# Branch A of a fused encoder block: 64 row products against two groups of seven block products, merged by accumulating DMA

## The chip, the core and the metric

One NeuronCore of a Trainium2 chip runs the whole layer in one launch. The metric is the time of one execution in microseconds (us) on the device. The engines are TensorE (PE, matmul; PEld is its weight load), VectorE (DVE), ScalarE (ACT), GpSimd (POOL) and SyncE (SP), which only issues DMAs. Each engine works through its own list of instructions in order; they meet at semaphores only.

## What is computed

One encoder layer, 512 tokens of width 1024, float32. One projection of the normalised input feeds three token mixers: A (sliding-window attention, 16 heads), X (cross-attention into 256 memory tokens) and P (pooling). Then

```
ya = oa @ w_branch_a          # (512 x 1024) @ (1024 x 1024)
yx = ox @ w_branch_x          # (512 x 512) @ (512 x 1024)
yp = op @ w_branch_p          # (512 x 512) @ (512 x 1024)
merged = gate_a * ya + gate_x * yx + gate_p * yp
x = x + rms_norm(merged @ w_out, norm_mix_post)
h = rms_norm(x, norm_ffn_pre)
x = x + rms_norm((silu(h @ w_gate) * (h @ w_up)) @ w_down, norm_ffn_post)
```

The gates are sigmoids of 3 x 1024 further columns of the input projection. The change concerns `ya` and the merging.

## The kernel before

**Precision.** Every float32 operand is kept as two float32r parts: `hi` is a rounded copy (ScalarE, `Copy`), `lo` is the rest (VectorE, subtract). A product is three matmuls, hi*hi, hi*lo and lo*hi (`three`, L1944). So each weight tile passes SP (load), ScalarE (`split_hi`, L469), VectorE (`split_lo`, L482) and TensorE.

**The stream.** `plan` (L92) lists `steps`: memory rows, k, v, q, qx, pin, 12 gate tiles, P tiles 0 to 3, X tiles 0 to 7, then A tiles 0 to 3, P tiles 4 to 7, A tiles 4 to 7. A step of A is one tile of 128 output channels by 512 tokens, 8 slices of 128 inputs, so 24 matmuls of 512 columns. A step of P or X is two tiles of 4 slices each. `stream` is the order of weight loads: two entries are one 1 MB chunk, in one of two `raw` buffers (`load_chunk`, L623); the chunks of the output projection (`out`) are mixed in between. Splits run up to two steps ahead (`stream_upto`, L495); `wait_split_free` (L413) says when a destination is free.

**Units.** Twelve attention units (8 of A, 4 of X) are laid over steps 15 to 38, two steps each: scores, maxima, exponentials, `normalise` (L1413), transposes (L2075) and output (L2085).

**Late groups.** Twelve of the gate tiles (A 0 to 7 and P 4 to 7) are computed in three late groups ahead of step A0 (44, `LATE`, L66) by a seven-product scheme: a 2 x 2 block product with 7 block products instead of 8 (`products`, L80; `late_product`, L2105). Its operands are blocks of the weights (A11 to A22) and sums of them (S1 to S4, VectorE, `late_weight_sum` L1469), blocks of the tokens (B11 to B22) and sums of these (T1 to T4). The T sums are made by POOL (L845 to L862) from `hT_hi` and `hT_lo`; POOL starts on them when the last A unit and the last `map` tile are done. ScalarE splits them in `token_hi` (L967) at steps A0-4 and A0-3. The intermediate results U1, U2 and U3 are copied from PSUM by ScalarE (`late_keep`), and VectorE adds them to the block results (`late_block_out`). One block product is 2 x 4 x 3 = 24 matmuls of 256 columns. The feed-forward uses the same scheme.

**Merging.** For each tile VectorE multiplies the PSUM tile by its gate (`merge`, L1437, into `part`) and adds it to the running sum in `gates` (L1451). For an A tile this is the last addition: ScalarE then makes `mrg_hi` (L951) and VectorE `mrg_lo` (L1460), two steps later in their lists.

**Output projection.** L2187: token rows t = 0 to 3; in row t = 0 each slice k waits for its weights `wo_hi[k]`, `wo_lo[k]` and for `mrg_split`; 6 matmuls of 512 columns per k and t. SP reloads x into `x1` when all tiles are done (L712), then the two gains and the first feed-forward chunks.

**POOL.** Besides the T sums: the pooling mixer (L834 to L840, four groups), the row norms (`inverse_rms`), and a few sums later. It issues no DMA in this kernel.

The lines that matter for memory: `op_hi` lies at 176 KB and `op_lo` at 184 KB of each partition (read by the P tiles), `late_sum` at 192, `part` and `late_U2` at 200, `late_U1` at 204, `gates` at 72 to 96, `hT_hi` and `hT_lo` at 40 to 72.

Of the kernel before, what the change touches and what calls it, by code (L numbers as in the profile page):

```python
# [65 lines left out]
LATE = (("a", 0), ("a", 4), ("p", 4))  # L66
# [25 lines left out]
def plan():  # L92
# [17 lines left out]
    steps += [[("a", j)] for j in range(4)] + halves("p", 4) + [[("a", j)] for j in range(4, KT)]  # L110
# [15 lines left out]
def encoder_block(nc, x, x_t, mem_t, g_mix_pre, g_mix_post, g_mem, w_in, rel_bias, sinks, w_mem_kv, w_pool_map,  # L126
# [9 lines left out]
    A0 = steps.index([("a", 0)])  # L136
# [67 lines left out]
    out_at = [40, 48, 56, 64, 72, 80, 88, 196]  # L204
    wo_hi = [sb(f"wo_hi{k}", a, [P, D], F32R) for k, a in enumerate(out_at)]
    wo_lo = [sb(f"wo_lo{k}", a + 4, [P, D], F32R) for k, a in enumerate(out_at)]
# [64 lines left out]
    rel_dram = nc.dram_tensor("rel_scratch", [A_HEADS, 192], F32, kind="Internal").ap()  # L271

# [6 lines left out]
    with ExitStack() as ctx:  # L279
# [14 lines left out]
        for n, t in enumerate(tiles):  # L294
# [7 lines left out]
            if A0 <= step < A0 + 4:  # L302
                b = (step - A0 + 2) % 4
# [18 lines left out]
        x_again = [sem(f"x_again{i}") for i in range(TT)]  # L322
# [18 lines left out]
        sigmoid_ready, mixed_ready, mrg_hi_done, mrg_split = (sem(n) for n in ("sigmoid_ready", "mixed_ready", "mrg_hi_done", "mrg_split"))  # L341
# [10 lines left out]
        late_sigmoid = sem("late_sigmoid")  # L352
        ops_hi, ops_split, product_done = sem("ops_hi"), sem("ops_split"), sem("product_done")
# [13 lines left out]
        def chunk_halves(first):  # L367
# [7 lines left out]
            else:  # L375
# [6 lines left out]
                if t == "a":  # L382
                    v, col = wa_v, P * i
                elif t == "gate":
# [28 lines left out]
        def wait_split_free(eng, s):  # L413
# [6 lines left out]
            elif kind == "out" and n < 4:  # L420
                eng.wait_ge(late_done, OPS * len(LATE))
            elif kind == "out":
                eng.wait_ge(tile_full, len(tiles))
                eng.wait_ge(mrg_split, KT)
            elif kind == "ffn" and n < 3:
                eng.wait_ge(tile_full, len(tiles))
# [169 lines left out]

        def both(name):

            return pair["CDAB".index(name)][:, :, 0:2 * P]
# [12 lines left out]
        def _(sp):  # L612
# [97 lines left out]
            for c in range(late_chunk + 1, last_out + 1):  # L710
                load_chunk(c)
            sp.wait_ge(tile_full, len(tiles))  # L712
            for t in range(TT):
                sp.dma_start(x1[:, t, :], x[P * t:P * t + P, :]).then_inc(x_again[t], 16)
# [61 lines left out]
        def _(pool):  # L776
# [46 lines left out]
            pool.wait_ge(pads_ready, 6)  # L823
            for g, w in enumerate(POOL_WINDOWS):
# [17 lines left out]
            pool.wait_ge(o_full, A_UNITS)  # L842
            pool.wait_ge(tile_full, tile_no[("map", 3)] + 1)
# [6 lines left out]
            def token_diff(dst, a, b):  # L850
# [11 lines left out]
                .then_inc(late_t_made, 1)  # L862

# [23 lines left out]
        def _(act):  # L887
# [61 lines left out]
            def merged_hi(j):  # L949
                act.wait_ge(mixed_ready, j + 1)  # L950
                act.activation(mrg_hi[:, j, :], mix_slot(j), ACT.Copy).then_inc(mrg_hi_done, 1)  # L951
# [91 lines left out]
            for s in range(NS):  # L1043
# [6 lines left out]
                if s >= 2 and steps[s - 2][0][0] == "a":  # L1050
                    merged_hi(steps[s - 2][0][1])
# [45 lines left out]
            for j in (KT - 2, KT - 1):  # L1097
                merged_hi(j)
# [212 lines left out]
        def _(dve):  # L1311
# [125 lines left out]
            def merge(t):  # L1437
# [4 lines left out]
                if kind == "a" or (kind == "p" and j >= 4):  # L1442
                    dve.wait_ge(late_sigmoid, 2 * [k for k, at in LATE].index(kind) + (2 * (j // 4) + 2 if kind == "a" else 2))
                else:
                    dve.wait_ge(sigmoid_ready, (j if kind == "p" else 4 + j) // 2 + 1)
                onto = kind == "a" or (kind == "p") == (j >= 4)
                dst = part[:, :] if onto else gate_slot(kind, j)
                dve.tensor_tensor(dst, bk(bank_of[n]), gate_slot(kind, j), ALU.mult).then_inc(tile_merged, 1)
                if onto:
                    dve.wait_ge(tile_merged, merged_no[t])  # L1450
                    ins = dve.tensor_tensor(mix_slot(j), mix_slot(j), part[:, :], ALU.add)  # L1451
                    if kind == "a":
                        ins.then_inc(mixed_ready, 1)
                        dve.wait_ge(mixed_ready, j + 1)
                    else:
                        link(ins)

            def merged_lo(j):
                dve.wait_ge(mrg_hi_done, j + 1)
                dve.tensor_tensor(mrg_lo[:, j, :], mix_slot(j), mrg_hi[:, j, :].bitcast(F32), ALU.subtract)\  # L1460
                   .then_inc(mrg_split, 1)

# [130 lines left out]
            for s in range(NS):  # L1593
# [9 lines left out]
                if s >= 2 and steps[s - 2][0][0] == "a":  # L1603
                    merged_lo(steps[s - 2][0][1])
# [29 lines left out]
                if s >= 1 and not A0 - 6 < s <= A0:  # L1634
                    for t in steps[s - 1]:
# [4 lines left out]
                        elif t[0] in "axp":  # L1640
# [13 lines left out]
                if s == MEM_TURNS + 1:  # L1654
                    for e in range(E_X, E_V):
# [6 lines left out]
                        ins.then_inc(turned_split, 1)  # L1662
            for t in steps[NS - 1]:
                merge(t)
            for j in (KT - 2, KT - 1):
                merged_lo(j)
# [24 lines left out]
            for t in range(TT):  # L1691
                if t >= 1:
                    h2_lo(t - 1)
                dve.wait_ge(x_again[t], 16)
# [248 lines left out]
        def _(pe):  # L1943
# [16 lines left out]
            def tile(t, s, midway=None):  # L1960
# [13 lines left out]
                if A0 <= s < A0 + 4:  # L1974
# [13 lines left out]
                if kind in ("a", "p", "x"):  # L1988
                    xhi, xlo = {"a": (oa_hi, oa_lo), "p": (op_hi, op_lo), "x": (ox_hi, ox_lo)}[kind]
                else:  # L1990
                    xhi, xlo = hT_hi, hT_lo
                if kind == "a":
                    pe.wait_ge(o_split, A_UNITS)
# [139 lines left out]

# [253 lines left out]
```

## Time and profile before

| | us |
|---|---|
| runs of the kernel | 778.16, 779.55, 780.31 (median 779.55) |
| the profiled execution | 778.36 |
| its span in the profile | 776.6 |
| TensorE busy | 767.9 (99%) |
| VectorE, ScalarE, POOL busy | 575.4, 377.5, 90.7 |
| DMA | 85.76 MB, mean 110 GB/s |

The span is 1.8 us shorter than the execution's own time; start and end lie around it. In a record of a matmul the duration includes the pipeline's length, so the pace is read from the distance of two starts, not from the duration.

### The profile page before, as it was taken

The page shows a single profiled execution, that of the slowest core. Times are in us where ns is not written, and L with a number is a line of the kernel's source. Part 1 is how long each engine was busy: PE and PEld are TensorE (multiplying, and loading weights), DVE is VectorE, ACT ScalarE, POOL GpSimd, SP SyncE. Part 2 cuts the span into 40 slices and gives each one's busy share as a digit, 9 for nine tenths or more (in the row PEclk, how much of TensorE's full clock was granted, in tenths as well). Part 3 has the DMA queues.
Part 4 walks back from the last instruction along what each step waited for, and adds up shares of the span by engine and source line. Part 5 has one row for each costly group of instructions (what it writes and reads, how often), then busy time and mean ns, then how long its engine had stood idle before and what let it go on. Part 6 is the DMA issues. An engine that isn't in the chain of part 4 may idle for free.

```text
span 776.6 us, 11895 instructions
## 1 busy us (share of the span) xinstructions
PE 767.9 (99%) x4670; PEld 677.6 (87%) x4670; DVE 575.4 (74%) x643; ACT 377.5 (49%) x598; POOL 90.7 (12%) x139
## 2 busy tenths in 40 slices
PE   8999999999999999999999999999999999999997
PEld 7888778777877899988888999999999999888885
DVE  6666566676745788867655598888888888999897
ACT  7733445444337445553243565544445445675462
POOL 5120001334910000000001110000011110000002
PEclk9999999999999999999999999999999999999999
DMA  8862213213211333244371013333333346214102
GB/s 298 304 199 73 90 56 100 63 55 98 66 54 59 105 109 107 84 136 151 120 270 55 5 52 110 109 108 108 108 108 108 108 135 216 108 57 166 50 1 108
DMA packets 68070, 85.76 MB, mean 110 GB/s; under 512 B 3504, under 2 KB 57536, under 8 KB 68032
## 3 DMA queue, kind: packets, MB, share of 16 engines
q1 hardware_dynamic: 67568, 84.71, 33.3%
q8 instruction: 26, 0.43, 0.2%
q10 hardware_dynamic: 464, 0.53, 0.2%
q14 instruction: 12, 0.10, 0.0%
HBM read 83.12 MB, written 2.11 MB: 110 GB/s over the span
## 4 chain that ended last, share of the span: by engine, by line
PE 98%; DMA 1%; ACT 0%; DVE 0%; DVEq 0%; issue 0%; POOLq 0%; SPq 0%; POOL 0%; ACTq 0%
PE pair L1950 91%; PE pair L2082 1%; PE pair L2064 1%; PE pair L2096 1%; PE pair L2071 1%; PE pair L2101 1%; DMA memT_in<-in_mem 1%; PE pair L1957 0%; PE pair L1978 0%; PE pair L2032 0%; PE pair L2160 0%; PE pair L2171 0%; PE pair L2177 0%; DVE x L1677 0%; ACT square L901 0%; DVEq L279 0%
## 5 line engine op out<-in xcount | busy, mean ns | idle before, releaser
L1950 PE MATMUL pair<-hT_hi,w_hi 128*128 128x512 f32 x240 | 98.1, 409 | 0.0
L493 DVE TENSOR_TENSOR w_lo<-raw,w_hi 128x1024 fp32r<-128x1024 f32 x52 | 70.5, 1356 | 35.6 <-ACT w_hi L480 35.5
L1950 PE MATMUL pair<-hT_hi,w_lo 128*128 128x512 f32 x240 | 93.8, 391 | 0.0
L1950 PE MATMUL pair<-hT_lo,w_hi 128*128 128x512 f32 x240 | 93.6, 390 | 0.0
L1950 PE MATMUL pair<-T_hi,op_lo 128*128 128x256 f32 x320 | 90.6, 283 | 0.0
L1950 PE MATMUL pair<-T_hi,op_hi 128*128 128x256 f32 x320 | 90.6, 283 | 0.0
L1950 PE MATMUL pair<-T_lo,op_hi 128*128 128x256 f32 x320 | 90.6, 283 | 0.0
L480 ACT ACTIVATE w_hi<-raw 128x1024 fp32r<-128x1024 f32 x52 | 54.8, 1056 | 49.9 <-PE pair L1950 30.8
L1950 PE MATMUL pair<-B_hi,op_lo 128*128 128x256 f32 x240 | 67.9, 283 | 0.0
L1950 PE MATMUL pair<-B_hi,op_hi 128*128 128x256 f32 x240 | 67.9, 283 | 0.0
L1950 PE MATMUL pair<-B_lo,op_hi 128*128 128x256 f32 x240 | 67.9, 283 | 0.0
L1950 PEld LDWEIGHTS pair<-T_hi,op_hi 128*128 128x128 f32 x320 | 61.4, 192 | 0.0
L1950 PEld LDWEIGHTS pair<-T_hi,op_lo 128*128 128x128 f32 x320 | 61.4, 192 | 0.0
L1950 PEld LDWEIGHTS pair<-T_lo,op_hi 128*128 128x128 f32 x320 | 61.4, 192 | 0.0
L1950 PEld LDWEIGHTS pair<-hT_hi,w_hi 128*128 128x128 f32 x240 | 45.1, 188 | 10.4 <-issue 1.0
L1950 PEld LDWEIGHTS pair<-hT_hi,w_lo 128*128 128x128 f32 x240 | 45.0, 188 | 9.8
L1950 PEld LDWEIGHTS pair<-hT_lo,w_hi 128*128 128x128 f32 x240 | 45.1, 188 | 9.7 <-issue 1.0
L800 POOL TENSOR_SCALAR meansq<-part_meansq 128x1 f32<-128x1 f32 x16 | 5.7, 356 | 358.1 <-ACT square L901 357.8
L1950 PEld LDWEIGHTS pair<-B_hi,op_hi 128*128 128x128 f32 x240 | 46.1, 192 | 0.0
L1950 PEld LDWEIGHTS pair<-B_hi,op_lo 128*128 128x128 f32 x240 | 46.1, 192 | 0.0
L1950 PEld LDWEIGHTS pair<-B_lo,op_hi 128*128 128x128 f32 x240 | 46.1, 192 | 0.0
L1147 ACT ACTIVATE U<-pair 128x512 f32<-128x512 f32 x30 | 17.9, 598 | 57.6 <-PE pair L1950 57.6
(273 smaller groups left out, 2051.1 us busy)
## 6 DMA issues: line engine op xcount, KB each, us to landing
raw<-in_w_in SPq DMA_DIRECT2D x42, 512.0 KB, 4.8
raw<-in_w_ffn_up SPq DMA_DIRECT2D x22, 512.0 KB, 4.8
raw<-in_w_ffn_gate SPq DMA_DIRECT2D x22, 512.0 KB, 4.2
W<-in_w_ffn_down SPq DMA_DIRECT2D x8, 1024.0 KB, 5.0
raw<-in_w_branch_a SPq DMA_DIRECT2D x8, 512.0 KB, 4.0
raw<-in_w_out SPq DMA_DIRECT2D x8, 512.0 KB, 3.7
raw<-in_w_ffn_down SPq DMA_DIRECT2D x6, 512.0 KB, 4.2
raw<-in_w_mem_kv SPq DMA_DIRECT2D x4, 512.0 KB, 6.9
```

The lines of the kernel that those rows point to most:

```text
L480: eng.activation(hi, src, ACT.Copy).then_inc(weights_hi, 1)
L493: eng.tensor_tensor(lo, raw_view(s), hi.bitcast(F32), ALU.subtract).then_inc(weights_split, 1)
L800: link(pool.tensor_scalar(meansq[:, n:n + 1], part_meansq[:, c:c + 1], 1.0, EPS, ALU.mult, ALU.add))
L1147: act.activation(kept[u][:, :, :], both("A"), ACT.Copy).then_inc(kept_ready, 1)
L1950: ins = pe.matmul(dst, a, b, start=first and n == 0, stop=last and n == 2, skip_group_check=onto)
L2064: ins = pe.matmul(scores[:, pr // 2, at:at + KEYS], q[lo:lo + 64, 2 * a + pr % 2, ch, :, :].rearrange("p j t -> p (j t)"), k_dup[lo:lo + 6 ...
L2071: ins = pe.matmul(scores[:, i // 2, at:at + N_MEM], qx[:, a, P * i:P * i + P], mk[:, a, :], start=True, stop=True)
L2082: ins = pe.transpose(turned[:, at // 4, P * (at % 4):P * (at % 4) + P], probs[:, i, :], ident[:, :])
L2096: ins = pe.matmul(bk(O_BANK)[64 * half:64 * half + 64, 2 * P * c:2 * P * c + 2 * P], v_c[:, 2 * b + c, 64 * a:64 * a + 64], probs[:, i:i + ...
L2101: ins = pe.matmul(bk(O_BANK), mv[:, m, a, :], probs[:, 4 * m:4 * m + 4, :], start=(m == 0), stop=(m == MT - 1))
```

## The change

Branch A leaves the list of steps. P tiles 4 to 7 become the last steps, and `ya` is computed behind them in two groups (`BRANCH`, output channels 0 to 511 and 512 to 1023) of seven block products.

- The weights' sums S1 to S4 are made once, in DRAM, by POOL's DMAs: four copies, then four accumulating DMAs, two of them behind the pooling mixer. Signs are arranged so that only additions are needed.
- The tokens' sums T1 to T4 of `oa` are made by VectorE in `late_t` (steps 31 to 34), stored to DRAM by POOL, and loaded again by SP during the last late group. POOL's own T sums for the late groups come behind the stores.
- The operands are loaded block by block into four buffers `br_raw` (512 KB each), split by ScalarE and VectorE, in an order that is written out by hand along with everything else of this stretch.
- Each of the eight results (C11, C22, C21, C12 of a group) is formed by VectorE, multiplied by its gate, and added into `gates` by an accumulating DMA from SBUF to SBUF that POOL issues, each after the one before has landed. `merged_hi` and `merged_lo` then work on these blocks.
- The splits of the output projection's weights move: k=0 behind P tiles, k=1 to 5 into the second group, k=6 behind the last accumulation, k=7 behind the last `merged_lo`.

The diff, cut to its core:

```diff
-LATE = (("a", 0), ("a", 4), ("p", 4))
+LATE = (("p", 4), ("a", 0), ("a", 4))
+BRANCH = (0, 4)
+BLOCK_ORDER = ("C11", "C22", "C21", "C12")
-    steps += [[("a", j)] for j in range(4)] + halves("p", 4) + [[("a", j)] for j in range(4, KT)]
+    steps += halves("p", 4)
-    for c, at in ((1, n - 2), (0, n - 6)):
-        stream[at:at] = [("out", 2 * c), ("out", 2 * c + 1)]
-    stream += [("out", k) for k in range(4, KT)]
+    stream += [("out", k) for k in range(KT)]
+    br_raw = [sb(f"br_raw{i}", a, [P, 4, 2 * P]) for i, a in enumerate((192, 196, 184, 188))]
+    br_kept = {"U1": sb("br_U1", 204, [P, 2, 2 * P]), "U2": sb("br_U2", 202, [P, 2, 2 * P])}
+    br_kept["U3"] = br_kept["U1"]
+    br_out = {"C11": br_kept["U1"], "C22": sb("br_C22", 200, [P, 2, 2 * P]), "C21": br_kept["U3"], "C12": br_kept["U2"]}
+    out_at = [(80, 84), (72, 76), (40, 48), (44, 52), (56, 64), (60, 68), (196, 200), (88, 92)]
...
+            elif kind == "out" and n == 6:
+                eng.wait_ge(br_mixed, 16 * 8)
+                eng.wait_ge(br_split, 2 * OPS)
             elif kind == "out":
-                eng.wait_ge(tile_full, len(tiles))
-                eng.wait_ge(mrg_split, KT)
+                eng.wait_ge(mrg_split, 8)
...
+            def load_branch(n):
+                g, m = divmod(n, OPS)
+                name = products()[m][1]
+                if n < 2:
+                    sp.wait_ge(late_split, OPS * len(LATE))
+                elif n < 4:
+                    sp.wait_ge(tile_full, len(tiles))
+                else:
+                    sp.wait_ge(br_split, n - 3)
...
+                sp.dma_start(br_raw[n % 4][:, :, :], src).then_inc(block_ins[n % 4], 16)
+            sp.wait_ge(tok_stored, 64)
+            sp.wait_ge(late_done, OPS * len(LATE) - 3)
+            for b in TOKEN_SPLITS:
+                sp.dma_start(br_t[b][0][:, :, :], br_tok[b].rearrange("p (k n) -> p k n", k=4)).then_inc(tok_in, 16)
+            load_branch(0)
+            load_branch(1)
+            load_chunk(late_chunk + 2)
+            for n in range(2, 2 * OPS):
+                load_branch(n)
...
+            for name, a in (("S1", "A21"), ("S3", "A11"), ("S2", "A11"), ("S4", "A12")):
+                pool.dma_start(br_summed(name), br_block(a)).then_inc(br_copied, 16)
+            pool.wait_ge(br_copied, 64)
+            for name, b in (("S1", "A22"), ("S3", "A21")):
+                pool.dma_start(br_summed(name), br_block(b), accum_op=ALU.add, max_dma_last_dim=4096).then_inc(br_added, 16)
...
+            for b in range(4 * len(BRANCH)):
+                pool.wait_ge(br_gated, b + 1)
+                if b:
+                    pool.wait_ge(br_mixed, 16 * b)
+                pool.dma_start(br_part(gates, b), br_out[BLOCK_ORDER[b % 4]][:, :, :], accum_op=ALU.add).then_inc(br_mixed, 16)
...
+            def br_keep(g, u):
+                act.wait_ge(br_done, OPS * g + {"U1": 1, "U2": 3, "U3": 5}[u])
+                if u == "U3" or g:
+                    act.wait_ge(br_mixed, 16 * (4 * g + {"U1": -1, "U2": 0, "U3": 1}[u]))
...
+                act.activation(br_kept[u][:, :, :], both("A"), ACT.Copy).then_inc(br_kept_ready, 1)
+            def merged_hi(b):
+                act.wait_ge(br_mixed, 16 * b + 16)
+                act.activation(br_part(mrg_hi, b), br_part(gates, b), ACT.Copy).then_inc(mrg_hi_done, 1)
```

The order of ScalarE's list (VectorE's follows the same pattern, with the block results between):

```diff
+            br_operand_hi(0) ; br_token_hi("T2") ; br_token_hi("T1") ; br_operand_hi(1) ; br_operand_hi(2)
+            br_operand_hi(3) ; br_token_hi("T3") ; out_hi(0) ; br_keep(0, "U1") ; br_operand_hi(4) ; br_token_hi("T4")
+            br_operand_hi(5) ; br_keep(0, "U2") ; br_operand_hi(6) ; merged_hi(0) ; br_operand_hi(7) ; br_keep(0, "U3")
+            br_operand_hi(8) ; br_operand_hi(9) ; merged_hi(1) ; br_operand_hi(10) ; merged_hi(2) ; br_keep(1, "U1")
+            br_operand_hi(11) ; merged_hi(3) ; br_operand_hi(12) ; out_hi(1) ; br_keep(1, "U2") ; br_operand_hi(13)
+            merged_hi(4) ; out_hi(2) ; out_hi(3) ; br_keep(1, "U3") ; out_hi(4) ; out_hi(5) ; merged_hi(5)
+            merged_hi(6) ; out_hi(6) ; merged_hi(7) ; out_hi(7)
```

TensorE runs `branch_product` 14 times ahead of the output projection, in the order P1, P2, P6, P5, P7, P4, P3. P6 and P7 add onto the PSUM bank of P1 and wait for U1 and U2 to be kept; P3 adds onto that of P5 and waits for C22. In the output projection, row t = 0 waits for `mrg_split` 1, 3, 5 and 7 at k = 0, 2, 4 and 6, row t = 2 for 8.

## Rows read from the trace of the kernel before

**Rows 1.** The page: busy time, share of the span, instructions of each engine; chain by engine.
```profile
PE 767.9 (99%) x4670; PEld 677.6 (87%) x4670; DVE 575.4 (74%) x643; ACT 377.5 (49%) x598; POOL 90.7 (12%) x139
...
PE 98%; DMA 1%; ACT 0%; DVE 0%; DVEq 0%; issue 0%; POOLq 0%; SPq 0%; POOL 0%; ACTq 0%
```

**Rows 2.** The chain that ended last, in order of time: start us, us, what.
```profile
212.63 0.87 PE pair L2082 x8
...
247.83 162.81 PE pair L1950 x954
```

**Rows 3.** Busy time by stretch; then clock, DMA share, GB/s.
```profile
275.00:335.30 60.30, 60.30 (x505) 60.30 (x504) 51.03 (x51) 29.35 (x33) 0.00 (x0) 1.00 0.33 106
335.30:389.80 54.50, 54.50 (x243) 45.14 (x243) 36.04 (x43) 18.73 (x21) 0.00 (x0) 1.00 0.40 135
389.70:400.70 11.00, 11.00 (x49) 8.79 (x48) 7.37 (x8) 4.53 (x5) 0.00 (x0) 1.00 0.87 297
```

**Rows 4.** Timeline of TensorE: start us, us, instruction.
```profile
274.89 0.28 PE L1950 MATMUL pair<-hT_hi,late_op_hi 128*128 128x256 f32 x1
...
335.36 0.40 PE L1950 MATMUL pair<-oa_hi,w_hi 128*128 128x512 f32 x1
...
389.79 0.39 PE L1950 MATMUL pair<-wo_hi,mrg_hi 128*128 128x512 f32 x1
```

**Rows 5.** Busy time by stretch, columns as in rows 3: during the units.
```profile
72.00:98.00 26.00, 26.00 (x141) 20.53 (x139) 15.37 (x26) 12.08 (x40) 0.00 (x0) 1.00 0.26 81
```

**Rows 6.** Timeline of POOL from 140 us on.
```profile
148.29 3.02 POOL L834 TENSOR_TENSOR pooled<-pooled 128x512 f32<-128x512 f32 x2 [11.33 <-PE pair L1978]
...
194.05 5.74 POOL L847 TENSOR_TENSOR late_T<-hT_hi,hT_lo 128x1024 f32<-128x1024 f32 x2 [6.95 <-PE pair L1978]
...
213.98 3.23 POOL L861 TENSOR_TENSOR late_T<-late_T,late_T 128x1024 f32<-128x1024 f32 x1
401.93 0.19 POOL L800 TENSOR_SCALAR meansq<-part_meansq 128x1 f32<-128x1 f32 x1 [184.72 <-ACT square L901]
```

**Rows 7.** The page: DMA issues, KB each, us to landing.
```profile
raw<-in_w_in SPq DMA_DIRECT2D x42, 512.0 KB, 4.8
```

**Rows 8.** Timeline of VectorE, units 9 and 10.
```profile
205.04 2.15 DVE L1410 TENSOR_SCALAR neg_max<-row_max 128x4 f32<-128x4 f32 x1
...
209.40 2.26 DVE L1423 TENSOR_TENSOR probs<-probs,inv_denom 128x1024 f32<-128x1024 f32 x1
...
220.30 0.17 DVE L1410 TENSOR_SCALAR neg_max<-row_max 128x4 f32<-128x4 f32 x1
...
222.68 1.22 DVE L1423 TENSOR_TENSOR probs<-probs,inv_denom 128x1024 f32<-128x1024 f32 x1
```

**Rows 9.** Landing of L621 (320 to 390 us), L771 (result), L714 (x); one issue.
```profile
DMA to landing us min/median/max: 3.2/3.8/4.6
...
DMA to landing us min/median/max: 2.1/2.1/2.1
...
DMA to landing us min/median/max: 3.3/5.4/7.2
...
343.37 0.93 SPq L621 DMA_DIRECT2D raw<-in_w_branch_p  x2
```

**Rows 10.** Timelines of ScalarE, then VectorE; in brackets the idle time before and its end.
```profile
254.35 1.99 ACT L973 ACTIVATE late_T_hi<-late_T 128x1024 fp32r<-128x1024 f32 x2
...
329.80 0.60 ACT L977 ACTIVATE late_U<-pair 128x512 f32<-128x512 f32 x1 [2.32 <-PE pair L1950]
...
348.32 1.06 ACT L480 ACTIVATE w_hi<-raw 128x1024 fp32r<-128x1024 f32 x1 [1.09 <-DMA raw<-in_w_branch_p]
...
392.97 3.90 ACT L480 ACTIVATE wo_hi<-raw 128x1024 fp32r<-128x1024 f32 x4 [0.84 <-DVE mrg_lo L1460]
...
390.77 0.69 DVE L1451 TENSOR_TENSOR gates<-gates,part 128x512 f32<-128x512 f32 x1
...
394.06 4.63 DVE L493 TENSOR_TENSOR wo_lo<-raw,wo_hi 128x1024 fp32r<-128x1024 f32 x4 [1.21 <-ACT wo_hi L480]
```

More of the change, by code:

```diff
@@ L1441, in merge @@
                 dve.wait_ge(tile_full, n + 1)
[L1442 to L1443 removed]
+                if kind == "p" and j >= 4:
+                    dve.wait_ge(late_sigmoid, 2)
                 else:
                     dve.wait_ge(sigmoid_ready, (j if kind == "p" else 4 + j) // 2 + 1)
[L1446 removed]
+                onto = (kind == "p") == (j >= 4)
                 dst = part[:, :] if onto else gate_slot(kind, j)
@@ L1450, in merge @@
                     dve.wait_ge(tile_merged, merged_no[t])
[L1451 to L1460, printed above, removed]
-                   .then_inc(mrg_split, 1)
+                    link(dve.tensor_tensor(mix_slot(j), mix_slot(j), part[:, :], ALU.add))
@@ L1662, in _ @@
                         ins.then_inc(turned_split, 1)
+                if TOKENS_AT <= s < TOKENS_AT + 4:
+                    token_sums(s - TOKENS_AT)
+                if s == A0:
+                    br_operand_lo(0)
+                    br_token_lo("T2")
+            br_token_lo("T1")
+            br_operand_lo(1)
             for t in steps[NS - 1]:
                 merge(t)
-            for j in (KT - 2, KT - 1):
-                merged_lo(j)
+            br_operand_lo(2)
+            br_operand_lo(3)
+            br_token_lo("T3")
+            out_lo(0)
+            br_operand_lo(4)
+            br_token_lo("T4")
+            br_block_out(0, "C11")
+            br_operand_lo(5)
+            br_operand_lo(6)
+            merged_lo(0)
+            br_operand_lo(7)
+            br_block_out(0, "C22")
+            br_operand_lo(8)
+            br_block_out(0, "C21")
+            br_operand_lo(9)
+            merged_lo(1)
+            br_block_out(0, "C12")
+            br_operand_lo(10)
+            merged_lo(2)
+            br_operand_lo(11)
+            merged_lo(3)
+            br_block_out(1, "C11")
+            br_operand_lo(12)
+            out_lo(1)
+            br_operand_lo(13)
+            merged_lo(4)
+            out_lo(2)
+            out_lo(3)
+            br_block_out(1, "C22")
+            out_lo(4)
+            br_block_out(1, "C21")
+            out_lo(5)
+            merged_lo(5)
+            br_block_out(1, "C12")
+            merged_lo(6)
+            out_lo(6)
+            merged_lo(7)
+            out_lo(7)
+            done += KT
             def gained(t, h, n, number, y=y):
@@ L2132, in late_product, with branch_product @@
                 ins.then_inc(late_done, 1)
+            def branch_product(n):
+                g, m = divmod(n, OPS)
+                name, a, b, bank = products()[m]
+                pe.wait_ge(br_split, n + 1)
+                if name == "P1":
+                    if g:
+                        pe.wait_ge(br_kept_ready, 3 * g)
+                    else:
+                        pe.wait_ge(late_kept_ready, 3 * len(LATE))
+                        pe.wait_ge(o_split, A_UNITS)
+                if name == "P2" and g:
+                    pe.wait_ge(br_blocks, 4 * g - 3)
+                if name == "P5":
+                    if g:
+                        pe.wait_ge(br_blocks, 4 * g)
+                    else:
+                        pe.wait_ge(tile_merged, merged_no[tiles[-1]])
+                if name == "P6":
+                    pe.wait_ge(br_kept_ready, 3 * g + 1)
+                if name == "P7":
+                    pe.wait_ge(br_kept_ready, 3 * g + 2)
+                if name == "P3":
+                    pe.wait_ge(br_blocks, 4 * g + 2)
+                if g == 0 and b[0] == "T":
+                    pe.wait_ge(late_t_split, TOKEN_SPLITS.index(b) + 5)
+                (whi, wlo), xhi, xlo = br_op[n % 4], br_token(b, True), br_token(b, False)
+                fresh = name not in ("P6", "P7", "P3")
+                for i in range(2):
+                    for k in range(4):
+                        ins = three(both(bank)[:, i, :], whi[:, k, P * i:P * i + P], wlo[:, k, P * i:P * i + P],
+                                    xhi[:, k, :], xlo[:, k, :], fresh and k == 0, k == 3, onto=not fresh)
+                ins.then_inc(br_done, 1)
             def warm_up(n, bank):
```

227 lines of the change are left out of this document (189 added, 38 removed).

## The prediction

> **What bounds the kernel now.** I read the page first: TensorE is busy for 767.9 of 776.6 us and 98% of the chain that ended last is its own work [rows 1]. So only two things move the time: the matmul time in the stretch that is changed, and new idle time in front of a matmul. The chain in order of time shows 954 matmuls without a gap from 247.83 to 410.64 [rows 2]. This stretch holds the late gate groups, branch A, the last P tiles and the first row of the output projection. The granted clock there is 1.00 [rows 3]. VectorE is busy for 36.0 of 54.5 us and ScalarE for 18.7 [rows 3]: there is room, but both work through a fixed order, so the order decides.
>
> **What the change can gain.** The late groups run from 274.89 to 335.36: 60.47 us for 3 x 7 x 24 = 504 matmuls of 256 columns, 0.120 us each, so a block product takes 2.88 us. From 335.36 to 389.79 there are 240 matmuls of 512 columns, 0.2268 us each [rows 4]. Branch A is 8 x 8 x 3 = 192 of these: 43.5 us. Afterwards it is 2 x 7 x 24 = 336 of the short ones: 40.3 us. The gain is **3.2 us**, 0.41% of the time, and any wait of TensorE is taken from that. Counting 0.3% (2.3 us) as what a measurement can tell from no change, "faster" needs waits of less than 0.9 us in total.
>
> **What is moved ahead of 335 us, each at nothing, with its cover.**
> Weight sums: about 59 us POOL issues four 1 MB copies inside DRAM and waits for them, then two adds. Copies read and write 8 MB. Weight loads use 0.26 of the DMA engines at that time [rows 5]. At 100 GB/s the copies would last 80 us, to 139; POOL's next work starts at 148.29 [rows 6]. A weight load of 512 KB lands in 4.8 us [rows 7] and is issued two steps or more (14 us) before its split, so even a doubled landing is hidden. Without that cover each late chunk would cost TensorE its lateness.
> Token sums: eight VectorE operations of 1.2 us at steps 31 to 34 (185 to 217 us), in front of `normalise`. Before, unit 9's `normalise` ended at 211.66 and its transposes began at 212.63 [rows 2, 8]: only 1.0 us. But there VectorE was slowed by POOL's adds: the 2.26 us `normalise` takes 1.22 in unit 10, the 2.15 us `neg_max` 0.17 [rows 8]. POOL's adds now move behind the stores, so 3.0 us come back against 2.4 us of token work per step. Cost nothing.
> POOL's own chain for the late groups ran 194.05 to 217.21, 23.2 us [rows 6]. It now waits for the fourth sum (about 217) and the stores (5 us), so it runs from 222 to 246; ScalarE first wants its result at 254.35 [rows 10]. 8 us of slack; if it were gone, ScalarE's weight splits behind that wait would be late next. LATE's new order swaps equal groups. The `x_again` rename costs nothing. SP loads four token sums (2 MB) and operands 0 and 1 from about 328; P1 needs them only at 346.2 and P6 at 352.
>
> **The stretch from 335 us on.** P tiles 4 to 7 now come first: 48 x 0.2268 = 10.9 us, to 346.24. P1 and P2 follow to 352.0. Then:
>
> First wait, **P6**. Operands 2 and 3 go to `br_raw` at 184 to 192, where `op_lo` lies, so SP waits for the last P tile (its record ends 0.16 after its slot, 346.4). Loads there land 3.2 to 4.6 us after issue, median 3.8 [rows 9]; a pair issued at 343.37 let ScalarE start at 348.32, 4.95 later [rows 9, 10]. So operand 3 lands at about 351.4. ScalarE then does, in this order, operand 3, T3, output row 0 and only then keeps U1: 1.0 us each for the first three and 0.6 for U1 [rows 10]. U1 is there at 355.0; P6 adds onto the same PSUM bank and waits for it: **3.0 us**. With the fastest landing (3.2) still 1.5 to 2.3. Everything queued behind on ScalarE (operands 4, 5) keeps its lead.
>
> **The merging.** The last additions (0.69 us on VectorE [rows 10]) become eight accumulating transfers of 256 KB from SBUF to SBUF, issued by POOL one after the other, each after the previous landed. ScalarE waits for them in `merged_hi`, and its buffers U1, U2 and U3 wait as well. No row shows such a transfer. Nearest rows: a 256 KB store alone lands in 2.1 us; 512 KB loads in this stretch in 3.2 at least; the same under a burst in 5.4, up to 7.2 [rows 9]. The accumulation reads both operands, so its traffic is that of 512 KB; I take **3.2 us**, keep 2.1 and 5.4 as ends.
> The Trainium skill (DMA: Bandwidth & Descriptors, section Anatomy of one DMA) gives 2.0 us plus bytes over 436 GB/s for a GpSimd transfer, which would be 2.6 us here, an estimate. Collectives: The Full Stack (section The bandwidth ceiling) speaks against the change: a reducing transfer needs two source reads, an estimate of 3.2 us by the first rule. No row here shows either.
>
> I went through the orders written out for ScalarE and VectorE with 1.06 us for a ScalarE split (next start after 0.95: four take 3.90), 1.22 for a VectorE one (next after 1.14: four take 4.63) and 0.69 for a half one [rows 10]. With 3.2 us per transfer: the first group needs no further wait. In the second, C11 is gated at 379.4, landed at 382.6, split at 383.3; output rows 2 and 3 follow, then U3 at 385.7; VectorE makes C22 at 387.2. P3, which overwrites that bank, could start at 386.8: **0.4 us**. The products end at 390.15.
> Output projection, row 0: k=6 needs `wo_hi[6]` at 196 and 200 KB, where C22 and raw operands lie, so its split waits for all eight transfers. C22 is gated at 388.0; three transfers in a row end at 397.6; two splits end at 399.9. TensorE wants it at 390.15 + 6 x 1.36 = 398.3: **1.6 us**. k=7 waits for the last `merged_lo`, then two more splits, 402.9 instead of 401.3: **1.6 us**. Before, the splits of output rows 0 to 3 lay far ahead and the last four took 392.97 to 398.7 [rows 10], without a gap.
> Later rows, SP's loads of x (issued at 390.0 before and at 390.3 after) and the feed-forward are as before.
>
> **Sum.** -3.2 + 3.0 + 0.4 + 1.6 + 1.6 = **+3.4 us**. The profiled execution took 778.36 us (span 776.6); it would take 781.8. The median of the runs shown is 779.55, 1.2 above it, so the forecast is **783.0 us**. With 2.1 us per transfer only the P6 wait is left: -0.2, 779.4. At 2.6 us the sum is +0.1. At 3.2 and above every further us costs 8, since eight transfers follow each other and ScalarE waits in order: 4.6 gives +14.6, 5.4 gives +21.
>
> **Rivals.**
> A, no change that can be told: transfers take 2.1 to 2.9 us (-0.2 to +1.0), time 779.4 to 780.6. For it: the store's 2.1 us for the same bytes [rows 9]. Against: that store reads one source beside an idle DMA, while here SP moves operands. The 2.6 us of the Trainium skill (DMA: Bandwidth & Descriptors) would end here too.
> B, faster: U1 isn't late, because operands 2 and 3 land by 347.9, and transfers take under 2.5 us; then the whole 3.2 us stays, 776.3. It decides at the P6 wait: below 0.9 us it is faster. Against: no load in the stretch landed in under 3.2 us [rows 9].
> C, much slower: transfers take 4 us or more, because the two sources cost more than I count or because the burst of x, which held 297 GB/s from 389.7 to 400.7 [rows 3], meets the last three. At 4.0 the sum is +9.8 (789.4), at 5.0 +17.8 (797.4). TensorE then waits at P6, P7 and P3 of the second group too, and POOL's part of the row norms (first at 401.93 [rows 6]) is queued behind the last transfer.
> D, the early part: weight sums or POOL's late chain are late. Each us beyond 254 costs one; I see 8 us of slack, so it is in the tail of the range.
>
> **Chances.** Forecast (transfers of 2.9 to 3.9 us, +1.0 to +9) 0.38; A 0.27; B 0.06; C 0.26; D 0.03. A and the lower edge of the forecast lie within 0.3%: same 0.32. Faster 0.06, slower 0.62. The range leaves out B's better half and C above about 4.7 us per transfer: 778.2 to 795.0. The forecast's own range is 780.6 to 788.6.
>
> **What would show it.** In the trace after: P products at 0.120 us per matmul and 336 of them; a gap of TensorE after the second product with ScalarE's U1 as its end, 2 to 3.5 us; POOL-issued transfers landing in about 3.2 us; a gap near output k=6 and k=7 ended by VectorE's `wo_lo`. POOL's late chain near 222 to 246 with no gap of TensorE before 346. I am wrong in kind if the first gap is missing, wrong in size if transfers take another time; the weights' sums are wrong if a gap shows before 335.

## The result, and the profile after the change

| | before | after |
|---|---|---|
| median, us | 779.17 (778.16 to 780.31, 4 runs) | 802.44 (801.90 to 804.15, 4 runs) |
| ratio | | 1.0302, 95% interval 1.028 to 1.0324 |
| span of the profiled execution, us | 776.6 | 799.9 |
| granted TensorE clock, mean of the span | 0.998 | 0.988 |

The changed kernel is 23.3 us slower. The forecast was 783.0 us with a range of 778.2 to 795.0. The direction was right, the size was not, and the time lies above the range. Two later executions, of 2694 us in experiment 8 and of 1958 us in experiment 10, were slow for a reason that is not known and are left out of the times given there.

The page, busy time and chain by engine, the lines that answer to [rows 1]:

```profile
PE 771.0 (96%) x4814; PEld 686.3 (86%) x4814; DVE 596.2 (75%) x661; ACT 389.8 (49%) x614; POOL 110.7 (14%) x159
...
PE 48%; DMA 6%; DVE 4%; issue 1%; ACT 1%; SPq 0%; DVEq 0%; POOLq 0%; POOL 0%; ACTq 0%
```

TensorE's share of the chain fell from 98% to 48%. DMA and VectorE have appeared in it: TensorE no longer sets its own pace. Where it waited is in the list of waits of TensorE, up to the end of output row 0 (us in total, times, longest):

```profile
PE pair L2211 <- DVE wo_lo L515: 11.7, 1, 11.7
PE pair L2211 <- ACT br_U L1067: 3.4, 1, 3.4
PE pair L2211 <- DVE br_C L1667: 3.1, 2, 1.5
PE pair L2211 <- DVE br_op_lo L1622: 2.9, 1, 2.9
```

All of it lies behind 351 us; ahead of 346 us the list holds no wait that the kernel before doesn't have. The engines named here (VectorE, ScalarE) are only the last to arrive, and for the wait before P6 the name is the wrong one: P6 needs operand 2, whose `lo` was done at 352.8, and U1. `br_op_lo` is operand 3; what ended just ahead of P6 is ScalarE's copy of U1 (TensorE's row, then ScalarE's):

```profile
354.92 0.55 PE L2211 MATMUL pair<-br_T_hi,late_op_hi 128*128 128x256 f32 x1 [2.92 <-DVE br_op_lo L1622]
```
```profile
354.24 0.57 ACT L1067 ACTIVATE br_U<-pair 128x512 f32<-128x512 f32 x1
```

For the other three lines the name is right, but the engine named had itself been late. What it had waited for is one step back, in the waits of ScalarE between 330 and 430 us:

```profile
ACT mrg_hi L1071 <- DMA gates<-br_U: 23.5, 5, 10.5
ACT mrg_hi L1071 <- DMA gates<-br_C: 11.2, 2, 6.3
...
ACT wo_hi L502 <- DMA gates<-br_U: 3.7, 1, 3.7
```

ScalarE stood for 38 us in front of `merged_hi` and one output split, each time until an accumulating transfer had landed. The chain in order of time shows the transfers one by one (start us, us, what; six of the eight are in it; the fourth and fifth took 3.8 and 4.0), and the end of the stretch:

```profile
360.10 5.92 DMA gates<-br_U
...
370.51 5.75 DMA gates<-br_C
...
376.80 3.80 DMA gates<-br_U
...
397.53 4.22 DMA gates<-br_C
...
402.29 10.61 DMA gates<-br_U
...
413.44 3.79 DMA gates<-br_U
...
417.30 1.06 ACT wo_hi L502
...
418.38 1.24 DVE wo_lo L515
...
419.67 2.93 PE pair L2211 x6
```

The transfer that lands undisturbed takes 3.8 us; the first two, beside operand loads, 5.9 and 5.8; the seventh, issued at 402.29 among the loads of x (399.8 to 401.6) and the gains and feed-forward weights behind them, 10.6. The windows (columns as in rows 3) show the burst, then the clock:

```profile
402.30:412.90 10.60, 5.65 (x25) 4.33 (x24) 1.98 (x3) 0.11 (x1) 1.19 (x1) 0.99 1.03 339
...
354.90:357.00 2.10, 2.08 (x10) 2.10 (x11) 2.10 (x3) 2.10 (x3) 0.00 (x0) 0.50 0.89 287
...
381.90:384.00 2.10, 2.10 (x10) 2.10 (x11) 1.30 (x2) 0.79 (x1) 0.43 (x1) 0.54 0.61 89
...
419.60:422.60 3.00, 2.93 (x6) 1.84 (x6) 1.83 (x3) 1.06 (x1) 0.00 (x0) 0.50 0.00 0
```

The second to fourth rows are the stretches right after TensorE's three longest waits (2.92, 3.40 and 11.72 us). The granted clock there is 0.50 to 0.54, the lower of its two levels (1.2 GHz), where the kernel before had 1.00 throughout [rows 3].

**Where the 23.3 us are**, by the distances of matmul starts. The last matmul of output row 0 starts at 400.7 in the kernel before and at 424.0 in the changed one:

| term | forecast | measured |
|---|---|---|
| 336 short matmuls for 192 long ones | -3.2 | -3.1 |
| wait before P6, group 0 | 3.0 | 2.9 |
| wait before P3, group 0 | 0 | 1.5 |
| wait before P6, group 1 (U1 behind the third transfer) | 0 | 3.4 |
| wait before P3, group 1 | 0.4 | 1.5 |
| output k=6 | 1.6 | 11.7 |
| output k=7 | 1.6 | 0 |
| matmuls at the lower clock behind the waits (1.5 + 1.6 + 1.6) | 0 | 4.7 |
| starts around the waits | 0 | 0.7 |
| sum | +3.4 | +23.3 |

(The last term is the rest. The terms add up in time, but not each is a loss of its own: of the slow matmuls only those in group 1 are, as shown further down.) Behind row 0 the two kernels run alike.

### The profile page after: what moved, and what is told of

Its sections match the earlier page's. It is cut to its first block, busy times and chain, and to the rows that moved or that the text cites. A ratio compares the mean times of both kernels' runs of the same rounds, so it can differ in the third digit from the quotient of the medians.

```text
span 799.9 us, 12289 instructions
## 1 busy us (share of the span) xinstructions
PE 771.0 (96%) x4814; PEld 686.3 (86%) x4814; DVE 596.2 (75%) x661; ACT 389.8 (49%) x614; POOL 110.7 (14%) x159
## 4 chain that ended last, share of the span: by engine, by line
PE 48%; DMA 6%; DVE 4%; issue 1%; ACT 1%; SPq 0%; DVEq 0%; POOLq 0%; POOL 0%; ACTq 0%
PE pair L2211 48%; DMA gates<-br_U 3%; DMA br_raw<-in_w_branch_a 1%; DMA gates<-br_C 1%; DVE late_op_lo L1622 1%; DVE br_T_lo L1628 0%; PE pair L2218 0%; ACT wo_hi L502 0%; DVE gates L1611 0%; DVE part L1608 0%; DVE wo_lo L515 0%; DVE late_gates L1718 0%; DVE late_op_lo L1686 0%; SPq L772 0%; DVE br_op_lo L1622 0%
## 5 line engine op out<-in xcount | busy, mean ns | idle before, releaser
L515 DVE TENSOR_TENSOR w_lo<-raw,w_hi 128x1024 fp32r<-128x1024 f32 x44 | 59.8, 1360 | 24.4 <-ACT w_hi L502 24.3
L502 ACT ACTIVATE w_hi<-raw 128x1024 fp32r<-128x1024 f32 x44 | 46.3, 1055 | 39.3 <-PE pair L2211 30.2
L2211 PE MATMUL pair<-bw_hi,ba_hi 128*128 128x512 f32 x112 | 43.6, 389 | 0.0
```

The source lines that it names most:

```text
L502: eng.activation(hi, src, ACT.Copy).then_inc(weights_hi, 1)
L515: eng.tensor_tensor(lo, raw_view(s), hi.bitcast(F32), ALU.subtract).then_inc(weights_split, 1)
L2211: ins = pe.matmul(dst, a, b, start=first and n == 0, stop=last and n == 2, skip_group_check=onto)
```

## The experiments

Two theories stood after this reading. **T**: the eight transfers are the loss, through ScalarE's and POOL's order; take them away and about 20 us go. **R**: the written order of ScalarE and VectorE is at fault (operands, output splits), and the transfers only land in time that is lost anyway. All ratios are against the kernel before, on the same chip.

**1. The sums made by VectorE.**

```diff
-                pool.dma_start(br_part(gates, b), br_out[BLOCK_ORDER[b % 4]][:, :, :], accum_op=ALU.add).then_inc(br_mixed, 16)
...
                 dve.tensor_tensor(out, out, br_part(late_gates, b), ALU.mult).then_inc(br_gated, 1)
+                dve.wait_ge(br_gated, b + 1)
+                dve.tensor_tensor(br_part(gates, b), br_part(gates, b), out, ALU.add).then_inc(br_mixed, 16)
```

> The eight accumulating transfers are replaced by eight VectorE additions of 0.69 us; all else is as in the changed kernel. Theory T (the time of the transfers, chained through POOL's turn and ScalarE's order, is the loss): TensorE keeps only the wait at the first P6 (2.9 us and some slow matmuls behind it), so 3.2 gained against about 4.4 to 5: 780 to 782 us. Rival R (the feed of operands and the splits are too slow for seven products in a row, the transfers only fill that time): above 792 us, with waits of TensorE ended by VectorE's splits in the second group.

Measured: 781.81 us (781.37 to 782.08), 1.0037 [1.0023, 1.0052]. Its waits of TensorE after 346 us are two:

```profile
PE pair L2208 <- issue: 2.9, 1, 2.9
PE pair L2208 <- DVE wo_lo L515: 1.3, 1, 1.3
```

The first is the wait before P6, the second the one at k=7. So 20.6 of the 23.3 us are the transfers (20.0 when each kernel is set against the runs of the kernel before on its own chip). T holds. R in its strong form, a feed too slow without the transfers, falls; what the written order adds while there are transfers is not separated by this run, since a transfer costs TensorE only where an engine's order waits for it.

**2. Plain copies instead of accumulation.** Merged then holds only the last term; the sums with the P and X parts are left out.

```diff
-                pool.dma_start(br_part(gates, b), br_out[BLOCK_ORDER[b % 4]][:, :, :], accum_op=ALU.add)                    .then_inc(br_mixed, 16)
+                pool.dma_start(br_part(gates, b), br_out[BLOCK_ORDER[b % 4]][:, :, :])                    .then_inc(br_mixed, 16)
```

> The eight transfers copy in place of accumulating, so the sums of the P and X parts are left out of merged; same bytes moved in, no second source. If the second source makes the transfer long, each falls from 3.8 us toward the 2.1 us of a plain store and the time to about 785 to 790 us. If the price is fixed (issue by POOL, landing), the transfers stay within 0.5 us and the time within 3 us of 802.

Measured: 793.31 us (2 runs), 1.0187 [1.0167, 1.0208]. The landing times of the eight transfers (min, median, max), here and in the changed kernel:

```profile
DMA to landing us min/median/max: 2.5/3.4/7.3
```
```profile
DMA to landing us min/median/max: 3.8/4.1/10.6
```

The expectation hit neither of its two ranges. The accumulation adds 1.3 us to an undisturbed transfer. Where operand loads follow 0.9 us after the issue it adds more: the first two transfers took 2.7 and 2.8 us as plain copies and 5.9 and 5.8 as accumulating ones. POOL also spends 0.72 us on issuing each, against 1.2. Without accumulation 9.1 us of the 20.6 go. The other 11.5 stay with a plain copy: they are the landing itself, and what runs beside it (the wait at k=6 is still 10.7 us, with 7.3 and 6.3 us for the last two copies).

**3. Not in turn.** Each of the eight lands on a count of its own; POOL waits only for the gate.

```diff
-                if b:
-                    pool.wait_ge(br_mixed, 16 * b)
-                pool.dma_start(br_part(gates, b), br_out[BLOCK_ORDER[b % 4]][:, :, :], accum_op=ALU.add).then_inc(br_mixed, 16)
+                pool.dma_start(br_part(gates, b), br_out[BLOCK_ORDER[b % 4]][:, :, :], accum_op=ALU.add).then_inc(landed(b)[0], 16)
...
-                act.wait_ge(br_mixed, 16 * b + 16)
+                act.wait_ge(*landed(b))
```

> Each transfer has a semaphore count of its own and POOL doesn't wait for the one before. Theory T with turn-taking as a good part of it: C21 no longer starts 4 us after its gate is applied, the U1 wait in the second group (3.4 us) goes, and the last three overlap: 790 to 796 us. If the single landing alone is what matters: 799 to 803.

**4. x loaded behind the merging.**

```diff
             sp.wait_ge(br_done, 2 * OPS)
+            sp.wait_ge(br_mixed, 16 * 8)
             for t in range(TT):
                 sp.dma_start(x1...
```

> SP loads x and the gains only when all eight transfers have landed. If the burst of x is what stretched the seventh transfer from 3.8 to 10.6 us, it comes back to 3.8 to 4.5, TensorE's wait at output k=6 falls from 11.7 to about 5 us, and the time to about 795 us, unless x is then late. If the long one has another cause, it stays near 10 us and the time gets worse by the later x.

Measured: 798.09 us for the third (1.0249 [1.0224, 1.0273]), 798.45 for the fourth (1.0253 [1.0228, 1.0279]), 2 runs each. The turns are worth some 4 us, less than expected: the wait for U1 in group 1 fell from 3.4 to 0.8 us, but those before the two P3 rose from 3.1 to 5.5. The burst of x is worth some 4 us too. In the third the last two transfers still took 10.0 and 9.5 us. In the fourth the last three landed in 4.37, 3.79 and 3.78 us, and the wait at k=6 fell from 11.7 to 5.1:

```profile
398.01 4.37 DMA gates<-br_C
...
402.92 3.79 DMA gates<-br_U
...
407.25 3.78 DMA gates<-br_U
```

So the meeting with the burst is shown as the cause of the 10.6 us. Of the 6.6 us that it frees at k=6 about 4 come back in time: the matmuls behind the wait run longer at the lower clock (3.0 us lost in place of 1.9), and the gains, loaded later, land at 421.6.

**5. Both together.** The edits of 3 and 4.

> The changed kernel with both of the remedies that were tried singly: each transfer on a count of its own and not in turn (alone: 798.1 us against 802.4, 4.3 less), and the loads of x behind the last transfer (alone: 798.5, 4.0 less). If the two losses are separate terms, they add: about 794. If they are one and the same loss (the seventh transfer, which is stretched because it starts among the loads of x), the second remedy brings nothing more: 797 to 798.5.

Measured: 794.39 us (2 runs), 1.0197 [1.0174, 1.022]. The two add. The waits at the output are down to 3.0 us, but those within the groups are not (5.3 us before the two P3, 2.9 before the first P6), and a wait of 2.1 us behind the row norm is new, since x and the two gains now come late (the second gain lands at 417.7).

**6. The first wait alone, transfers kept.** Operands 2 and 3 are loaded early, into 104 and 108 KB, VectorE splits operand 2 ahead of the last P tiles' merge, and U1 is kept ahead of T3.

```diff
+    br_first = {n: sb(f"br_first{n}", a, [P, 4, 2 * P]) for n, a in ((2, 104), (3, 108))}
...
                 elif n < 4:
-                    sp.wait_ge(tile_full, len(tiles))
+                    sp.wait_ge(late_done, OPS * len(LATE))
...
             br_operand_hi(3)
+            br_keep(0, "U1")
             br_token_hi("T3")
             out_hi(0)
-            br_keep(0, "U1")
```

> The changed kernel with its accumulating transfers, and only the first wait taken away (operands 2 and 3 sooner, U1 sooner). If the waits add up, 4.5 us less: 797.5. If the chain runs through VectorE and the transfers (C11 gated near 359.8 whatever TensorE does), P6's wait goes and the time stays within 1 us of 802.

Measured: 801.31 us, 1.029 [1.027, 1.0311]. The wait before P6 is gone, and the one before P3 of group 0 is 5.9 us in place of 1.5: P3 starts at 369.64, where the changed kernel had 369.63:

```profile
369.64 0.55 PE L2220 MATMUL pair<-oa_hi,late_op_hi 128*128 128x256 f32 x1 [5.88 <-DVE br_C L1676]
```

While transfers set the pace, a wait ahead of them costs nothing of its own.

**7. The same early part with the sums by VectorE.** First only with U1 ahead of operands 2 and 3 (e6), then with early operands and output k=7's `hi` at 192 KB (e8).

> Vector merging as in e1, and ScalarE keeps U1 ahead of operands 2 and 3. If the wait at P6 (2.9 us and 1.6 us of slow matmuls) is a loss of its own, the time falls by 4 us to about 778. If VectorE is the bound there (in e1 it idles only 3.7 us between 347 and 402), P6 starts about 2.4 us sooner, but the time falls by 1 to 2.5 us only, to 779.5 to 781, and the later block results (C22) become what TensorE waits for.

> Vector merging; operands 2 and 3 loaded 11 us sooner into free memory and split ahead of the last P tiles' merge; U1 kept ahead of T3; the last output row's hi part where nothing holds it back. No wait at the first P6. With VectorE as the bound: 777.5 to 779.5 us, level with the kernel before. Without such a bound: 775.5 to 776.5.

Measured: 781.27 us (1.0034 [1.002, 1.0048], 5 runs) and 779.96 us (1.0021 [1.0011, 1.0032], 10 runs). Both lie just above the ranges that went with VectorE as the bound. In e6 the wait of 2.9 us at P6 is gone and the time fell by 0.5 us only: waits for splits and for C22 came in its place, 4.7 us in all against 4.2 in e1. The windows from 346.5 to 405 us, of the kernel before, of the changed kernel and of e8, show what took over; the third busy time is VectorE's:

```profile
346.50:405.00 58.50, 58.50 (x258) 48.17 (x257) 38.59 (x46) 18.60 (x24) 0.93 (x3) 1.00 0.53 180
```
```profile
346.50:405.00 58.50, 49.12 (x358) 47.50 (x358) 42.58 (x48) 26.03 (x32) 8.42 (x7) 0.94 0.69 194
```
```profile
346.50:405.00 58.50, 55.12 (x397) 51.48 (x396) 52.53 (x62) 30.99 (x40) 0.94 (x3) 1.00 0.62 203
```

VectorE rose from 38.6 to 52.5 of 58.5 us: there are operands and token blocks to split in place of plain weight tiles, eight results to form, and now the sums as well.

**8. The sums made by POOL** (as e8, `pool.tensor_tensor` in place of VectorE's addition).

> As e8, but the eight additions into gates are made by POOL instead of VectorE (128x512 from SBUF; POOL's 128x512 additions took 1.3 to 1.5 us before). If relieving VectorE of 8 x 0.6 us counts, 776 to 777.5 us. If POOL's additions slow VectorE's two-input operations down as they did at 205 to 212 us in the kernel before (1.2 us became 2.1 to 3.4), the gain is eaten: 778 to 780.

Measured: 782.22 us (3 runs), 1.0057 [1.0036, 1.0077], above both ranges. Six of the eight additions take POOL 2.14 us, against 0.69 on VectorE (the other two 1.3 and 1.6), and VectorE's operations beside them get longer:

```profile
369.37 2.14 POOL L961 TENSOR_TENSOR gates<-gates,br_U 128x512 f32<-128x512 f32 x1 [0.69 <-DVE br_U L1684]
```
```profile
363.19 0.68 DVE L1622 TENSOR_TENSOR mrg_lo<-gates,mrg_hi 128x512 fp32r<-128x512 f32 x1
...
370.28 1.77 DVE L1622 TENSOR_TENSOR mrg_lo<-gates,mrg_hi 128x512 fp32r<-128x512 f32 x1
```

The same VectorE operation takes 0.68 us alone and 1.77 beside POOL's.

**9. Transfers kept, everything around them arranged for them.** Experiments 3, 4 and 6, and output k=6 at 192 and 196 KB, so that no transfer stands before it; k=7 at 92 and 88 KB, behind seven merged blocks for `hi`; on VectorE operand 5 ahead of C11 and C12 ahead of the last splits. ScalarE's `merged_hi` stay where they were.

```diff
-    out_at = [..., (196, 200), (88, 92)]
+    out_at = [..., (192, 196), (92, 88)]
```

> The accumulating transfers kept, with everything around them rearranged: not in turn, loads of x behind them, operands 2 and 3 early, output k=6 split into 192 and 196 KB so that it waits for no transfer, k=7 split into 92 and 88 KB (behind the seventh and eighth merged block), VectorE's order C12 ahead of the last splits. Theory (what costs is TensorE waiting for output k=6 and k=7 behind the last transfers): C12 is gated at about 394, landed 398.5, its two splits and the split of k=7 end at 401, where TensorE wants k=7 at 399 to 400: about 783 us, +4 against the kernel before. Rival (transfers also hold up ScalarE's list within the groups, whatever is arranged behind them): waits before P7 and P3 of the second group stay and it takes 788 us or more.

Measured: 793.79 us (4 runs), 1.0195 [1.0172, 1.0218]. TensorE waits nowhere in the output's row 0, as wanted. But:

```profile
PE pair L2224 <- DVE br_C L1678: 8.9, 2, 7.3
PE pair L2231 <- DVE y L1493: 4.5, 1, 4.5
```

7.3 us before P3 of group 0, whose chain begins with a transfer of 5.9 us in front of `merged_hi(0)`; and 4.5 us for x and the gains, which now come behind the last transfer. The rival was right: freeing the end doesn't help, because ScalarE's list carries the transfers' length inside the groups too. No run moved `merged_hi` further back in that list, so how much of this the order could give back is open. No version with accumulating transfers that was tried came under 793.8 us.

**10. The sums by VectorE, its order mended.** Operand 5 ahead of C11, C12 ahead of the last splits, the output slots of 9 (e12); then also C22 as soon as U3 is kept, and the last split ahead of the last merged block (e14).

```diff
             br_token_lo("T4")
-            br_block_out(0, "C11")
             br_operand_lo(5)
+            br_block_out(0, "C11")
...
             br_block_out(1, "C21")
+            br_block_out(1, "C12")
             out_lo(5)
             merged_lo(5)
-            br_block_out(1, "C12")
             merged_lo(6)
             out_lo(6)
```

> The same arrangement with the sums made by VectorE, eight additions of 0.69 us in place of the transfers: the version of 779.96 us with three waits of TensorE taken away (operand 5 split ahead of C11; C12 formed ahead of the last splits; output k=6 and k=7 in buffers that wait for no merging or for the seventh block). If VectorE's order was the cause of those waits (0.86 + 0.82 + 0.53 us) and not its total load, 1.5 to 2.2 us go: 777.8 to 778.5 us, level with or just under the kernel before (778.6). If its load is the bound (52.5 of 58.5 us busy), the waits only move to the next split and the time stays at 779.5 to 780.

> The version of 779.03 us (e12) with what its trace still shows taken away: TensorE waits 1.29 and 0.73 us for C22 in front of P3, because VectorE forms C22 behind a split (group 0) and two splits (group 1) though U3 is kept 2 us earlier; here C22 comes ahead of them, and the last split (output k=7, now in 200 and 92 KB) ahead of the last merged block. If the order is the cause: both waits go, P3 of the second group ends 2.0 us earlier, and output k=7 waits for VectorE instead; VectorE's last split ends some 1.5 us earlier (0.95 us of idle time and the 0.6 us of the merged block no longer in front of it), so 777.3 to 778.0 us. If VectorE's total work is the bound, the two waits reappear at output k=4 to k=7 and the time stays at 778.7 to 779.3.

Measured: 779.03 us (12 runs), 1.0003 [0.9993, 1.0012], and 779.13 us (11 runs), 1.001 [1.0001, 1.0019]. e12 lies between its two ranges: the waits for `wo_lo` and `late_op_lo` were of VectorE's order and fell from 2.2 us (in e8) to 0.2, but those for C22 rose from 1.2 to 2.0, and the time fell by 0.9. In e14 it is the load, as its second range says: between 352 and 399.8 us VectorE stands still for 1.0 us in e12 and for 1.7 in e14. The waits of TensorE in e12, then in e14:

```profile
PE pair L2218 <- DVE br_C L1670: 2.0, 2, 1.3
PE pair L2218 <- DVE wo_lo L515: 0.2, 1, 0.2
```
```profile
PE pair L2218 <- DVE wo_lo L515: 1.1, 2, 0.7
PE pair L2218 <- DVE br_C L1670: 0.8, 1, 0.8
PE pair L2218 <- ACT br_U L1070: 0.5, 1, 0.5
```

What was taken from C22 stands at the output's splits and at U1: 2.2 us of waits became 2.4. No version was faster than the kernel before; the best is level with it.

## Why the prediction was right or wrong

**The bound and the gain: right.** The distance of two starts is 0.120 us for the short matmuls; the arithmetic gained 3.1 us of 3.2.

**The parts ahead of 335 us: right.** POOL's copies were issued from 59.4 us and its adds at 77.9, not at 139; the copies took 15.2 us of its waiting, so 100 GB/s was far too low a bound, and harmlessly so. The stores were issued by 215.0, POOL's chain for the late groups ran from 219.1 to 243.2 (forecast 222 to 246), and no wait of TensorE is there.

**The wait before P6: right.** 2.92 us against 3.0, U1 kept at 354.24 to 354.81 against 355.0. Behind it the matmuls started 0.21 us apart, at the lower clock, for 3.3 us, 1.5 us more that I had not counted. But experiment 6 shows that neither was a term to be added: without them the time fell by 1.1 us.

**The transfers: this step failed.** The step reads "I take 3.2 us", between the ends 2.1 and 5.4, and from it the orders of ScalarE and VectorE were worked out. An undisturbed transfer took 3.8 us. Beside operand loads the first two took 5.8 to 5.9, above my upper end; the seventh took 10.6. Nor did I count the 0.5 us between one landing and the next issue (376.80 after 376.29 in the chain). The 3.2 us was the fastest landing of a 512 KB load in [rows 9], taken for the two operands; that row's median, 3.8, was what the undisturbed transfer took, and by my slope it would have given +8.2. No row had an accumulation (1.3 us above a plain copy, 3 us and more beside loads), and I left the company of the transfer to a rival's chance instead of pricing it at each of the eight. The consequences I named under C came about: a wait at P6 of group 1 (3.4), at P3 (1.5) and at the output. That the first group needs no further wait was wrong as well: P3 waited 1.5 us there. My slope of 8 us per us of transfer was of the right order: the mean of the eight is 5.2 us, which by that rule gives +19.7. That this is near 23.3 is partly luck: the rule holds the early wait, which counts for little, and leaves out the lower clock. My sum also carries a slip of 0.2 us: by its own terms the products end at 390.0, not at 390.15.

Of the two pages that the prediction cited: the Trainium skill (DMA: Bandwidth & Descriptors, section Anatomy of one DMA) made 2.6 us for such a transfer, an estimate, and the plain copy's 2.5 us agrees. The Trainium skill (Collectives: The Full Stack, section The bandwidth ceiling) says that a reducing transfer needs two source reads, an estimate of 3.2 us; the direction agrees. The 3.8 us measured are 1.3 above the plain copy, where that estimate has 0.6.

**The output's k=6: mechanism right, size wrong.** I named the slot at 196 and 200 KB and its wait for all eight transfers. I had C22 gated at 388.0, it was at 397.2, because ScalarE and VectorE had already slipped by 9 us behind the transfers; three transfers then took 4.2 + 10.6 + 3.8 and two hand-overs, 19.7 us to the landing at 417.2, where I had 9.6. The k=7 wait did not show, because the slow matmuls of k=6 hid it: the split of k=7 ended at 422.55 and TensorE came to it at 422.61. At 0.227 us per matmul it would have been there at 421.0 and waited 1.5 us, near my 1.6.

**The lower clock: not in the sum at all.** 4.7 us in three places. Of these the 1.5 behind the first wait changed nothing later (experiment 6), and the 1.6 at k=6 stand in for the k=7 wait; the 1.6 in group 1, which lie on the chain, are a loss of their own. [Rows 3] show a clock of 1.00; the kernel before has no wait of TensorE in that stretch.

**The rivals.** C (0.26) is what happened, beyond its own price of +17.8 at 5.0 us. Its two conditions, the second source and the burst of x, are each shown (experiments 2 and 4). Rival A needed 2.9 us or less, which even a plain copy in this company did not keep (median 3.4). B's own condition was tried without transfers, in experiment 7: with U1 in time, the 3.2 us still did not stay, since VectorE, not the transfers, is then the bound. That was not among my rivals: I read its 36.0 of 54.5 us [rows 3] as room. The range failed because it cut off C above 4.7 us on the ground of a chance, while no row put a ceiling on a transfer that meets a burst; the x loads' own 7.2 us [rows 9] pointed the other way.

**What stays open.** How far the first transfer's 5.9 us is due to the operand loads was not tried alone; in all versions with accumulating transfers it took 5.8 to 6.3 us at this place, and as a plain copy at the same distance from the same loads 2.7. So the loads alone do not explain it. In the first 2.7 us after its issue the DMA engines were busy for only 0.16 of the time, against 0.52 with the plain copy, so it seems to begin later and to fall among the loads; no run tests that. That rearranging can't save the transfers is shown for the arrangements tried, not for all.

## What to carry to other kernels

A transfer of 256 KB between two engines' steps cost 3.8 us here where VectorE's addition cost 0.69; among a queue of bulk loads it cost almost three times that, and an engine that waits in order hands it on. Price each one in its place, by the row of a transfer in the same company, and put the upper end where the busiest such row is. Behind a long wait of TensorE count with matmuls at the lower clock (waits of 2.89 us and more were followed by 1.3 to 3.2 us of loss here), and ask whether anything later still waits for them. And before a saving on TensorE is counted, add up VectorE's work for the new scheme over the stretch: here it went from 38.6 to 52.5 of 58.5 us, and most of the 3.2 us gained on TensorE came back as waits for it.

## What the runs showed of the hardware that I had not expected

- An accumulating SBUF to SBUF transfer of 256 KB lands in 3.8 us undisturbed, a plain one in 2.5; POOL is held 1.2 us for issuing the one, 0.72 for the other.
- One such transfer issued among 4 MB of loads on another queue (x, two gains, the first feed-forward chunk) took 10.6 us; with these loads held back until it and the next had landed it took 3.8.
- Four copies of 1 MB inside DRAM, with the weight loads beside them, were done 18.5 us after their first issue (59.40 to 77.94).
- After waits of 2.9 and 3.4 us the granted clock was 0.50 and 0.54 over the next 2.1 us, and matmuls started 0.21 us apart for 3.3 to 3.6 us. Over all runs, waits within the two groups and output row 0 of 1.8 us and less were never followed by this, waits of 2.89 us and more always; between them it differed: after 2.56 and 2.72 us in experiment 5 the clock fell, after 2.87 us in the same run it stayed at 1.00.
- An addition of 128 x 512 takes POOL 2.14 us beside VectorE's work, 1.30 while VectorE stands still, where VectorE's own takes 0.69; a VectorE subtraction beside it goes from 0.68 to 1.77.
